# The opening of the expert rows in a one-core transformer kernel: early keys, four query slots in a second buffer, and a moved expert input

## What is computed

```python
def peer(h, w_query, sub_keys, expert_u, expert_v):
    q = (h @ w_query).reshape(B, S, PEER_HEADS, 2, PEER_HALF)      # 8 heads, 2 x 128
    sc = jnp.einsum('bshcd,hckd->bshck', q, sub_keys)              # 128 keys each
    sv, si = lax.top_k(sc, PEER_TOPK)                              # 16
    cand_s = (sv[..., 0, :, None] + sv[..., 1, None, :])...        # 16 x 16 pairs
    top_s, top_j = lax.top_k(cand_s, PEER_TOPK)                    # 16 of them
    eidx = ...; gate = softmax(top_s)                              # 128 experts per token
    u = expert_u[et]; v = expert_v[et]
    act = gelu(einsum('tnd,td->tn', u, xt)) * gt
    return einsum('tn,tnd->td', act, v)
```

## Time and profile before

| | |
|---|---|
| median of 3 runs | 1808.25 us (1805.47 to 1810.51) |
| profiled execution, device time | 1807.92 us |
| its span in the profile | 1806.1 us |
| busy: PE, DVE, ACT, POOL | 1535.2, 1052.3, 516.1, 521.2 us |
| moved by DMA | 486.91 MB, of these by POOL's queue 282.26 MB |
| granted TensorE clock, mean | 0.956 |

### The profile page before, as it was taken

How to read it: one execution, slowest core, us unless ns; L and a number is a source line. 1 busy time by engine, 2 the same in 40 slices (tenths; PEclk the granted TensorE clock), 3 DMA queues, 4 the chain that set the end, 5 groups by cost and what they waited for, 6 DMA issues and landing times.

```text
span 1806.1 us, 20370 instructions
## 1 busy us (share of the span) xinstructions
PE 1535.2 (85%) x8119; PEld 1079.7 (60%) x8119; DVE 1052.3 (58%) x1843; ACT 516.1 (29%) x722; POOL 521.2 (29%) x575
## 2 busy tenths in 40 slices
PE   4996998999999999989998986777776778886776
PEld 4876898879787998878875873222222223422224
DVE  3365655345485655445986589565655656654443
ACT  3333443334334454334222202111111112112111
POOL 3000000001000000000000165766666666666662
PEclk8998998999999999989999988999999989999999
DMA  9568656759665555554322499999999999999993
GB/s 356 204 251 251 227 178 219 209 193 303 256 254 176 174 185 187 186 181 146 121 101 97 178 408 418 382 372 370 371 356 354 376 374 360 375 383 367 362 367 155
DMA packets 115721, 486.91 MB, mean 270 GB/s; under 512 B 13120, under 2 KB 13280, under 8 KB 99248
## 3 DMA queue, kind: packets, MB, share of 16 engines
q0 software_dynamic: 78032, 282.26, 41.4%
q1 hardware_dynamic: 37600, 203.44, 31.5%
HBM read 484.18 MB, written 1.45 MB: 269 GB/s over the span
## 4 chain that ended last, share of the span: by engine, by line
PE 52%; POOL 16%; DVE 10%; DMA 10%; issue 8%; ACT 2%; another core or an unknown queue 2%; SPq 0%; POOLq 0%; DVEq 0%; ACTq 0%
PE G L957 18%; PE G L967 18%; POOL late L546 8%; PE M L1519 4%; PE T L957 4%; POOL mod L546 4%; DMA ring<-in_wpack 2%; POOL arena L546 2%; DVE wlo L1607 2%; DMA ybuf<-in_peer_u,mod 2%; POOL ybuf L546 2%; DMA arena<-in_peer_v,mod 1%; DMA late<-in_wpack 1%; PE G L1007 1%
## 5 line engine op out<-in xcount | busy, mean ns | idle before, releaser
L1607 DVE TENSOR_TENSOR wlo<-ring,whi 128x2048 fp32r<-128x2048 f32 x120 | 275.0, 2292 | 285.4 <-ACT whi L568 285.1
L568 ACT ACTIVATE whi<-ring 128x2048 fp32r<-128x2048 f32 x120 | 229.4, 1912 | 372.5 <-PE G L967 187.7
L1519 PE MATMUL M<-late,cB 128*128 128x512 f32 x480 | 239.6, 628 | 64.8 <-DMA late<-in_peer_v,mod 49.1
L2394 DVE SCALAR_TENSOR_TENSOR late<-late,G 128x1024 f32<-128x1024 f32 x128 | 153.6, 1219 | 111.8 <-DMA late<-in_peer_u,mod 104.8
L1519 PEld LDWEIGHTS M<-late,cB 128*128 128x128 f32 x480 | 85.7, 194 | 217.7 <-DMA late<-in_peer_v,mod 128.0
L892 ACT ACTIVATE cB<-consts,mod 128x128 f32<-128x128 f32 x240 | 85.5, 395 | 446.1 <-PE M L1519 183.0
L1519 PE MATMUL M<-mod,cB 128*128 128x512 f32 x240 | 128.9, 668 | 55.4 <-DMA mod<-in_peer_v,mod 37.2
L546 POOL DMA_INDIRECT late<-in_peer_v,mod x128 | 122.0, 953 | 67.4 <-issue 42.8
L546 POOL DMA_INDIRECT late<-in_peer_u,mod x128 | 121.1, 946 | 42.0 <-issue 36.9
L1519 PEld LDWEIGHTS M<-mod,cB 128*128 128x128 f32 x240 | 45.7, 208 | 134.6 <-DMA mod<-in_peer_v,mod 74.4
L957 PE MATMUL G<-hTl,whi 128*128 128x256 f32 x760 | 108.3, 286 | 0.0
(11 more groups left out here) (398 smaller groups left out, 2467.0 us busy)
## 6 DMA issues: line engine op xcount, KB each, us to landing
ring<-in_wpack SPq DMA_DIRECT2D x188, 1024.0 KB
late<-in_wpack SPq DMA_DIRECT2D x4, 1024.0 KB, 21.2
late<-in_peer_u,mod POOLq DMA_INDIRECT x128
late<-in_peer_v,mod POOLq DMA_INDIRECT x128
mod<-gate_rows POOLq DMA_DIRECT2D x6, 256.0 KB, 10.0
xs<-in_x SPq DMA_DIRECT2D x1, 1024.0 KB, 13.3
arena<-in_wsT POOLq DMA_DIRECT2D x1, 1024.0 KB, 10.0
mod<-in_bs POOLq DMA_DIRECT2D x1, 1024.0 KB, 14.4
```

Of the source, the lines that this page charges most:

```text
L568: nc.scalar.activation(whi[:, q % 2, :], ring[:, raw % RING, :], ACT.Copy).then_inc(hi_done, 1)
L1519: ins = nc.tensor.matmul(M[:, nb, :], diags[:, k % DIAGS, :], rowbufs[g % GBUF][:, nb, :], start=(n == 0), stop=(n == NSEL - 1))
L1607: V.tensor_tensor(wlo[:, q % 2, :], ring[:, raw % RING, :], whi[:, q % 2, :].bitcast(F32), ALU.subtract).then_inc(raw_free[raw % RING], 1)
L2394: V.scalar_tensor_tensor(out=row, in0=row, scalar=1.0, in1=G[:, t, :, :], op0=ALU.mult, op1=ALU.mult, accum_out=dots[:, t, n:n + 1]).then_ ...
```

## The change

1. The keys `skT` are loaded as soon as the conv branch's products are read, and the expert norm's gain in two halves, to places that are free then (`fgain`). The projection weights `wproj` are loaded before gather 32 and no longer before gather 0.
2. `peer_q` slots 4 to 7 leave the ring order. SP loads all four, in the order 6, 7, 4, 5, into `late` once the last split product has been made. The row buffers are laid out anew: 4 and 5 in `arena`, 6 and 7 in `ybuf`, 8 to 15 in the first 8192 values of `late`. Slot 6 lies over buffers 12 and 13, slot 7 over 14 and 15. Gathers 12 and 14 wait for the queries of slots 6 and 7, the load of `wproj` for all four. TensorE and ScalarE take the wide queries in the order 6, 7, 4, 5, and all scores from step 2 on behind them.
3. TensorE makes the head scores directly behind the transposes.
4. VectorE makes the first reciprocal and `expert_input(0)` before the last two column groups, and `expert_input(1)` in step 1.
5. ScalarE makes the exponential of step 1 and the gelu of step 0 behind all score copies. Two semaphore names of the modulation rows are shared now; that changes no order.

```diff
                 order += [(later, j) for j in range(count) if (later, j) not in order]
-            order += [(name, j) for j in (2 * i, 2 * i + 1) if name != "ada0z" and (name, j) not in order]
+            order += [(name, j) for j in (2 * i, 2 * i + 1)
+                      if name != "ada0z" and (name, j) not in order and not (name == "peer_q" and j >= 4)]
     return order
...
     return f"raw_free{h % RING}", h // RING + 1
+
+
+QUERY_ORDER = (0, 1, 2, 3, 6, 7, 4, 5)
+LATE_AT = {4: 8192, 5: 10240, 6: 4096, 7: 6144}
 
...
         relH = carve(modf, 4096, (H, TOK))
-        fgrow = carve(modf, 4352, (D,))
+        fgain = [carve(arena, 12288, (512,)), carve(modf, 9600, (512,))]
         logit = carve(modf, 6144, (H, TOK))
...
 
-        rowbufs = [carve(buf, 512 * k, (2, 512)) for buf, n in ((modf, 8), (late, 16)) for k in range(0, n, 2)]
+        rowbufs = [carve(modf, D * k, (2, 512)) for k in range(4)]
         rowbufs += [carve(arena, 10240 + k, (2, 512)) for k in (0, D)]
         rowbufs += [ybuf[:, t, :].rearrange("p (a n) -> p a n", a=2) for t in range(TT)]
+        rowbufs += [carve(late, D * k, (2, 512)) for k in range(8)]
         diags = cB
...
                 sp.dma_start(dst, slot_source(A["wpack"], name, j)).then_inc(raw_full[h % RING], 16)
+                if (name, j) == ("peer_q", 3):
+                    sp.wait_ge(split_used, SPLIT0["end"])
+                    for e in (6, 7, 4, 5):
+                        sp.dma_start(late[:, LATE_AT[e]:LATE_AT[e] + HALF],
+                                     slot_source(A["wpack"], name, e)).then_inc(sem("late_full"), 16)
                 if h == 2:
...
             load(clnb, A["conv_ln_b"].partition_broadcast(P), "l_cln")
-            pool.wait_ge(m_free, SPARE0["att"])
-            load(fgrow, A["ffn_norm_g"].partition_broadcast(P), "l_fg")
+            for i in range(2):
+                read_out(pool, "conv", i)
+            load(skT, A["skT"], "l_sk")
+            for nb in range(2):
+                load(fgain[nb], A["ffn_norm_g"][nb * 512:(nb + 1) * 512].partition_broadcast(P), "l_fg")
 
             for i in range(2):
                 read_out(pool, "out", i)
-            load(skT, A["skT"], "l_sk")
             load(ptT, A["pT"], "l_pt")
-            load(wproj, A["w_ple_proj"], "l_proj")
             for g, row in enumerate(GATHERS):
...
                     pool.wait_ge(sem(what), count)
+                elif g in (12, 14):
+                    pool.wait_ge(sem("late_free"), g // 2 - 5)
+                if g == SLICE:
+                    pool.wait_ge(sem("late_free"), 4)
+                    load(wproj, A["w_ple_proj"], "l_proj")
                 j = g % GBUF
...
                     act.wait_ge(sem("query_made"), e + 1)
+                elif e < 4:
+                    h = RAW["peer_q", 2 * e - 3]
+                    act.wait_ge(raw_free[h % RING], h // RING + 1)
                 else:
-                    h = RAW["peer_q", (1, 3, 4, 5, 6, 7)[e - 2]]
-                    act.wait_ge(raw_free[h % RING], h // RING + 1)
+                    act.wait_ge(sem("late_free"), QUERY_ORDER.index(e) - 3)
                 if e < 4:
...
             first_head()
-            for e in range(STEPS):
+            for e in QUERY_ORDER:
                 queries(e)
                 if e in (0, 1):
                     sub_scores(e)
                 elif e == 3:
                     gate_exp(0)
-                elif e == 5:
-                    gate_exp(1)
-                elif e in (6, 7):
-                    sub_scores(e - 4)
-            for q in range(SLICES, STEPS):
-                if q == 6:
-                    expert_gelu(0)
+            for q in range(2, STEPS):
                 sub_scores(q)
+            gate_exp(1)
+            expert_gelu(0)
             for q in range(STEPS):
...
                 t, s = divmod(q, SLICES)
-                pe.wait_ge(sem("query_read"), (1, 2, 6, 8)[min(q, 3)])
+                pe.wait_ge(sem("query_read"), (1, 2, 8)[min(q, 2)])
                 if q == 0:
...
 
-                w = raw(RAW["peer_q", slot])
+                if slot < 4:
+                    w = raw(RAW["peer_q", slot])
+                else:
+                    pe.wait_ge(sem("late_full"), 64)
+                    w = late[:, LATE_AT[slot]:LATE_AT[slot] + HALF].rearrange("p (k n) -> p k n", k=DC)
                 part = slice(0, TOK) if t is None else slice(t * P, (t + 1) * P)
                 return product(dst, lambda k: w[:, k, c * P:(c + 1) * P], lambda k: hT[:, k, part])
 
             def release(ins, slot):
 
-                ins.then_inc(raw_free[RAW["peer_q", slot] % RING], 1)
+                ins.then_inc(sem("late_free") if slot >= 4 else raw_free[RAW["peer_q", slot] % RING], 1)
 
             def bank_read(e):
-                pe.wait_ge(sem("query_read"), e - 1)
+                pe.wait_ge(sem("query_read"), QUERY_ORDER.index(e) - 1)
 
...
             x_turn(3)
+            head_scores()
             turned("norm5", 4)
             query(quarter(0, 2), 1, 0, 0)
-            head_scores()
             query(quarter(0, 3), 1, 1, 0).then_inc(sem("query_made"), 1)
...
                         sub_scores(1)
-            for e in range(4, STEPS):
+            for e in QUERY_ORDER[4:]:
                 bank_read(e)
                 for c in range(2):
                     ins = query(T[:, e % 2, c * TOK:(c + 1) * TOK], e, c)
                 release(ins, e)
-                if e >= 6:
-                    sub_scores(e - 4)
-            for q in range(SLICES, STEPS):
+            for q in range(2, STEPS):
                 sub_scores(q)
...
                 V.tensor_tensor(rbias[:, u, :], rbias[:, u, :], rgain[:, u, :], ALU.mult).then_inc(sem("row_made"), 1)
+
+            def expert_input(t):
+                for nb in range(2):
+                    n = slice(nb * 512, (nb + 1) * 512)
+                    link(V.scalar_tensor_tensor(out=G[:, t, nb, :], in0=xs[:, t, n], scalar=rstd[:, t:t + 1],
+                                                in1=fgain[nb], op0=ALU.mult, op1=ALU.mult))
 
...
                             block_read(V.tensor_tensor(xs[:, 1, 512:D], xs[:, 1, 512:D], G[:, b % 2, 1, :], ALU.add), "out", 1)
-                        if g == 2:
                             dve.wait_ge(sem("head_std"), 1)
                             V.reciprocal(rstd[:, 0:1], std[:, 0:1]).then_inc(sem("head_rstd"), 1)
-                    for i in range(2):
-                        read_out(dve, "out", i)
-                    dve.wait_ge(sem("head_rstd"), 1)
+                            for i in range(2):
+                                read_out(dve, "out", i)
+                            dve.wait_ge(sem("head_rstd"), 1)
+                            dve.wait_ge(sem("l_fg"), 32)
+                            expert_input(0)
                     dve.wait_ge(sem("norm_std"), n + 1)
...
                                            in1=i12[:, 1, h, :], op0=ALU.mult, op1=ALU.add).then_inc(sem("eidx_ready"), 1)
-                    if h == 0:
-                        dve.wait_ge(sem("l_fg"), 16)
-                        dve.wait_ge(sem("norm_rstd"), 6)
-                        for t in range(TT):
-                            expert_input(t)
                 link(V.tensor_copy(gmax[:, 0:HEADS], topv[:, 0:HEADS, 0]))
...
                         embed_add(0)
+                    if (q, n) == (1, 4):
+                        dve.wait_ge(sem("norm_rstd"), 6)
+                        expert_input(1)
                     expert_dot(t, s * SLICE + n)
```

9 lines of the change are left out of this document (2 added, 7 removed).

## The result

The changed kernel takes 1822.99 us (median of 12 runs, 1818.32 to 1827.63), the kernel before 1808.09 beside it (12 runs, 1801.93 to 1818.06): ratio 1.0080, 95% interval 1.0067 to 1.0093. That is 14.9 us slower, and above the range that the prediction gave. The profiled execution has a span of 1822.5 us against 1806.1.

The account below looks back on a forecast made before the run. The prediction took POOL's gathers and what frees its 16 row buffers as the bound, with VectorE limiting the opening. Gather 49 some 2.5 us later on 1807.92 gave 1810.4, forecast as 1810.5, range 1800 to 1816.

Parts of the forecast that it names:

- from slot 7's query to gather 48: Opening: slot 7's query ends at 1074.4, gather 14 goes at 1074.5, gather 48 at 1117.8.
- VectorE's chain: VectorE from row 14's landing through dots and selection: step 0 ends at 1107.9, 4.1 us later; gather 48 at 1117.8.
- First head 3.0 us earlier, gather 0 at 1031.4: VectorE starts the first head at about 1021.9 instead of 1024.94, so POOL's gather 0 goes 3.0 us earlier.
- Expert input hidden: VectorE's four multiplications, 3.14 us between the heads, move into waits and cost nothing; first selection ends about 6.1 us earlier.
- Gathers 12 and 14: POOL waits there for slots 6 and 7, some 20 and 5 us; gather 14 at 1074.5, 22 us late.
- 35 steps at 1.243 us: POOL from gather 14 to 49: 43.5 us plus 0.8 for the projection weights' load, gather 49 at 1118.8 against 1116.40.
- slack behind slot 7: TensorE's two wide queries behind slot 7 take about 15 us; slot 5's ends at 1089.5, gather 32 wants it at 1096.9.
- second slow stretch: Rival: TensorE gaps again before slot 7's query ends; half gives 1815.3, whole 1820; chance 0.18, shared with a starved opening.
- forecast of 2.4 us for the waits as such: Waits at gathers 12 and 14 put gather 49 at 1118.8 against 1116.40; POOL's former waits are all swallowed.
- The slow stretch does not come back: Rival: TensorE's 9.6 us of gaps vanish, slots 6 and 7 end at 1064.8, total 1800.9; chance 0.20.
- The step from gather 49 to the end: Expert stage behind the opening: same code and data, so it carries gather 49's shift one for one to the end.
- The sum: Whole kernel: profiled 1807.92 + 2.5 = 1810.4, the runs' median 1808.25 being 0.33 above the profiled time; forecast 1810.5.

Follow-up runs that it names:

- slots only: Changed kernel without early keys, gain and head scores and without the moved expert input; four early query slots, waits at gathers 12 and 14 and new order kept: ratio 1.0073.
- hold 4: Kernel before with only early keys, gain and head scores and moved expert input, plus gather 4 waiting for ScalarE's copy of step 1's score: ratio 1.0053.
- waits only: Kernel before plus only two POOL waits: gather 12 for slot 4's query, gather 14 for slot 5's: ratio 1.0121.

## Why the prediction was wrong

The step that failed is the one from slot 7's query to gather 48. The prediction let VectorE's chain run on to the end of step 0 and put its wait for ScalarE's gelu at nothing. In the changed kernel ScalarE came 12.1 us late to the last wide query and 4.1 us late to the last score, and VectorE stood 17.56 us for the gelu.

Point by point, with the changed kernel's trace on the chip of the result. Times in the span compare badly by themselves, since x was done 1.4 us earlier in this execution; counted from its last addition the forecast for gather 49 is 103.2 and the measured time 114.5, 11.3 us later:

- **First head 3.0 us earlier, gather 0 at 1031.4: right.** 15.7 us behind the last addition of x instead of 18.8.
- **Expert input hidden: right,** no wait was added by it. But the 6.1 us that VectorE was to gain went into its wait of 8.43 us for ScalarE's score copy. I had looked for starved engines on TensorE and VectorE and not on ScalarE, though its "remote" idle time of 7.54 us before 1070.45 was in the trace of the kernel before.
- **Gathers 12 and 14: right.** Forecast 1074.5 for gather 14, measured 1071.30 (58.9 and 57.1 behind the addition of x), with the waits of some 20 and 5 us (19.55 and 4.72).
- **35 steps at 1.243 us: the number came out by luck.** Gather 47 goes at 1116.85, and without the wait 49 would have gone at 1119.3, against the 1118.8 forecast. But gather 14 was 3.2 us earlier than forecast, and the steps from it took 48.0 us for 44.3: 3.13 of the difference are the wait ahead of gather 32, which the prediction didn't have.
- **VectorE's chain: wrong, and this is the step that failed.** Its last part said that ScalarE's last score copies "now lie ahead of the step's end; this frees some us". They do not lie ahead. The last wide query was copied 12.1 us late, TensorE's clock had fallen while it stood (some 0.9 us more for each score than at the upper level), the last score was copied 4.1 us late, its copy ended at 1118.50 + 0.69 = 1119.19, the gelu came at 1120.62, and VectorE, whose dots were done by 1103.4, waited 17.56 us. Gather 48 was forecast at 1117.8 and came at 1127.48, 9.7 us later, or 11.1 counted from x. The "slack behind slot 7", which I put against the rival of a second slow stretch, was counted from slot 5's end to gather 32 alone; the gelu behind the scores had little: on the chip without the gap it waits 4.09 us for VectorE.
- **The forecast of 2.4 us for the waits as such** doesn't hold even without the new order: alone they cost 22 us, by the same mechanism. POOL's pauses, which I counted as "swallowed" gain, were the times in which the other engines went on.
- **The rivals.** "A second slow stretch" was the right kind, on ScalarE instead of TensorE and behind slot 7 instead of ahead of it; it gave 1815.3 to 1820, and 1822.99 was measured. "The slow stretch does not come back" had 1064.8 for slots 6 and 7, 1109.2 for gather 49 and 7.3 us of gain. On the other chip slot 7's wait ends at 1063.93, gather 49 goes at 1108.36, and the kernel gains 10.0 us. Both of its times came true within 1 us there (counted from x both came 2 us earlier than it had them); I had asked whether the stretch comes back, and the answer differs between the two chips. No trace of the kernel before was taken on that chip, so how its own opening runs there is open.
- **The step from gather 49 to the end: right in kind.** 13.7 us there became 16.7 at the last gather. Over the first table the time lost by the ratio is 0.5 to 1.1 us for each us at gather 49 (slots only 13.2 for 18.2, hold 4 9.6 for 9.7, waits only 21.9 for 20.8).
- **The sum.** 1808.25 + 2.5 is 1810.75 and not 1810.5, and the former waits left out one of 3.29 us at gather 24. Neither changes the outcome.

Of the Trainium skill, "Runtime: NRT & Kernel Launch", Instruction fetch mechanics, says that the fetch is mostly hidden. On the chip with 1736 us the trace agrees, with no gap at a DMA share of 0.99; on the others it doesn't explain copies that come 10 to 34 us late. That the late thing is the fetch isn't shown. In the profile of the changed kernel the queues of kind "instruction" have 59 and 30 packets in the whole span,

```profile
q8 instruction: 59, 0.97, 0.2%
q14 instruction: 30, 0.25, 0.0%
```

and none of them lies between 1077 and 1125 us, where ScalarE's 18.39 us end. What ScalarE waits for, and what makes the chips differ, stays open.

## What to carry to other kernels

Where one engine issues a long row of transfers, look at what all the others do in its pauses before taking these away: here two waits for a buffer, added at an earlier place, cost 22 us instead of 2.5, and in their trace three short pauses have become one row of 34 gathers, behind which ScalarE goes on. Put what the issuer waits for next (here the gelu and the weights) ahead of work that can come later (six score copies) on every engine that it passes, so that a late engine costs less. Moving one of the two things alone, the gelu, brought 0.9 us at gather 49; interleaving the scores as well brought 3.9. And time a change of some tenths of a per cent on more than one chip, since this one is 0.8% slower on one and 0.6% faster on another.

## What the runs showed of the hardware

- The same program, the kernel before, takes 1808 to 1816 us on some chips and 1736 on others, 4% less, measured at different times (one of the slower chips gave 1815.76 and 1808.00 in two sets of runs). For the changed kernel the difference lies in the stage whose DMA engines are full: it issues 163 gathers in 228 us on the one and 184 on the other, at a granted clock of 0.96 and 1.00.
- On the slower ones ScalarE stands up to 32.5 us (waits only, before 1119.88) with work ready while gathers are issued without a pause, and in the opening mostly goes on 1.9 to 6.6 us after the last. TensorE issues one to four matmuls between gaps of 0.2 to 2.4 us in the same rows of gathers.
- TensorE's granted clock was 0.50 at 1090 to 1100 us in the changed kernel, behind 12.77 us in which it stood, and 0.72 at 1080 to 1090 on the other chip with idle times below 1 us between scores: eight small matmuls took 1.13 us at the upper level and 2.04 at the lower.
